# The gated quadrants of a convolution-and-MLP layer: TensorE transposes replaced by transposing transfers

## The reference

```
h = rmsnorm(x, mix_norm)
b, c, v = split(h @ conv_w_in, 3)              # 2048 -> 3 x 2048
u = c * v
y = causal depthwise convolution of u, 3 taps over the tokens
x = x + (b * y) @ conv_w_out
a = relu(rmsnorm(x, mlp_norm) @ mlp_w1)        # 2048 -> 8192
out = x + (a * a) @ mlp_w2                     # 8192 -> 2048
```

## Time and profile before

| what | value |
|---|---|
| median of 3 runs | 1902.61 us (1902.35 to 1905.46) |
| the profiled execution, its own time | 1902.01 us |
| its span | 1900.2 us |
| PE busy | 1892.1 us, 100% |
| DVE busy | 1678.3 us, 88% |
| ACT busy | 1036.5 us, 55% |
| mean busy share of the DMA engines | about 0.7 to 0.9 |
| median landing of a 1 MB weight load issued by SP | 7.5 us |
| PE transposes (L1328) | 392, of them 64 for GATED pairs |

### The profile page before, as it was taken

How to read it: one execution, slowest core, us unless ns; L and a number is a source line. 1 busy time by engine, 2 the same in 40 slices (tenths; PEclk the granted TensorE clock), 3 DMA queues, 4 the chain that set the end, 5 groups by cost and what they waited for, 6 DMA issues and landing times.

```text
span 1900.2 us, 22331 instructions
## 1 busy us (share of the span) xinstructions
PE 1892.1 (100%) x8540; PEld 1568.6 (83%) x8540; DVE 1678.3 (88%) x1500; ACT 1036.5 (55%) x1110; POOL 150.9 (8%) x242
## 2 busy tenths in 40 slices
PE   9999999999999999999999999999999999999999
PEld 8888888888888888888888888888888888888887
DVE  6689899898999898989989899898998889788878
ACT  6464564545558477586675866745444343334432
POOL 0100010000011111120110201100000000000000
PEclk9999999999999999999999999999999999999999
DMA  9774768749676976987968879699988878877783
GB/s 372 263 261 124 265 206 326 234 120 329 216 208 267 354 241 205 338 282 241 357 221 326 288 243 356 222 397 403 357 328 344 346 283 314 352 314 278 294 328 118
DMA packets 137306, 537.87 MB, mean 283 GB/s; under 512 B 27888, under 2 KB 31984, under 8 KB 112240
## 3 DMA queue, kind: packets, MB, share of 16 engines
q1 hardware_dynamic: 103072, 412.65, 56.7%
q0 software_dynamic: 33984, 123.75, 21.3%
q10 hardware_dynamic: 144, 0.04, 0.0%
HBM read 438.35 MB, written 94.37 MB: 280 GB/s over the span
## 4 chain that ended last, share of the span: by engine, by line
PE 68%; DMA 1%; ACT 0%; issue 0%; DVE 0%; SPq 0%; ACTq 0%
PE pair L1293 66%; PE pair L1328 1%; DMA raw<-in_turns 1%; SPq L410 0%; DVE raw L985 0%; ACT sum L695 0%; ACT quads L749 0%; DVE sum_l_mix L1022 0%; ACT ring L651 0%; ACT junk L759 0%; ACT quads L701 0%; DVE x L1100 0%; ACT act L769 0%; ACTq L650 0%; ACTq L360 0%
## 5 line engine op out<-in xcount | busy, mean ns | idle before, releaser
L1293 PE MATMUL pair<-ring,act 128*128 128x512 f32 x7728 | 1767.0, 390 | 1.5 <-issue 1.2
L1293 PEld LDWEIGHTS pair<-ring,act 128*128 128x128 f32 x7728 | 1446.2, 188 | 302.5 <-issue 4.1
L651 ACT ACTIVATE ring<-raw 128x1024 fp32r<-128x1024 f32 x659 | 696.4, 1060 | 798.3 <-PE pair L1293 512.1
L991 DVE TENSOR_TENSOR ring<-raw,ring 128x1024 fp32r<-128x1024 f32 x659 | 792.2, 1221 | 159.1 <-ACT ring L651 156.8
L985 DVE TENSOR_TENSOR raw<-raw 128x1024 f32<-128x1024 f32 x312 | 367.8, 1220 | 9.9 <-DMA raw<-in_turns 1.7
L518 POOL DMA_DIRECT2D spill<-stage x136 | 78.6, 617 | 488.2 <-ACT stage L774 372.8
L531 POOL DMA_DIRECT2D raw<-in_turns x56 | 50.4, 1053 | 701.2 <-DVE raw L985 701.2
L972 DVE TENSOR_TENSOR stage<-quads,stage 128x1024 fp32r<-128x1024 f32 x68 | 83.0, 1221 | 23.8 <-ACT stage L774 23.1
L1306 PE MATMUL pair<-ring,act 128*128 128x512 f32 x384 | 87.3, 389 | 0.0
L1306 PEld LDWEIGHTS pair<-ring,act 128*128 128x128 f32 x384 | 72.0, 188 | 14.9
L774 ACT ACTIVATE stage<-quads 128x1024 fp32r<-128x1024 f32 x68 | 71.5, 1051 | 15.9 <-DVE quads L889 6.2
(11 more groups left out here) (107 smaller groups left out, 527.8 us busy)
## 6 DMA issues: line engine op xcount, KB each, us to landing
raw<-in_turns SPq DMA_DIRECT2D x191, 1024.0 KB, 7.5
act<-spill SPq DMA_DIRECT2D x290, 512.0 KB, 6.8
spill<-stage POOLq DMA_DIRECT2D x136, 512.0 KB, 9.3
act<-act_kept SPq DMA_DIRECT2D x74, 512.0 KB, 7.0
raw<-in_turns POOLq DMA_DIRECT2D x56, 512.0 KB, 8.4
act_kept<-act POOLq DMA_DIRECT2D x28, 512.0 KB, 9.6
x_tok<-in_x SPq DMA_DIRECT2D x4, 1024.0 KB, 14.8
x<-mixed SPq DMA_DIRECT2D x8, 512.0 KB, 18.3
```

Source lines behind the costliest of these rows:

```text
L651: nc.scalar.activation(ring[g % RING][:, 0], raw[:, raw_of(v, s), 2 * (s % 2):2 * (s % 2) + 2, :], ACT.Copy).then_inc(hi_ready, 1)
L991: nc.vector.tensor_tensor(ring[g % RING][:, 1], raw[:, raw_of(v, s), 2 * (s % 2):2 * (s % 2) + 2, :], ring[g % RING][:, 0].bitcast(F32), A ...
L1293: mm = nc.tensor.matmul(bank, stationary, moving, start=(opens and k == 0 and n == 0), stop=(closes and k == NT - 1 and n == 2))
```

## The change

Both quadrants of a GATED pair are now turned over as the fourth quadrant of an UP pair is: planes of half words, a transposing transfer, and ACT puts the halves together, here straight into `u_pad`. PE does no transposes for GATED pairs. On ACT, `put_planes` comes at steps 4 and 6 of turns 2, 4, 8 and 10 (two instructions each), and `take_u` at steps 6 and 8 now waits for the transfer and has two instructions instead of one. At step 6 `take_u` of the first half comes before `put_planes` of the second. SP issues both transfers at the head of its list for the turn, each behind its planes. GATED pairs have planes of their own in the stage buffers. The read of x11 moves from SP's list of turn 31 (behind its first activation load) to the end of its list of turn 32.

```diff
 def by_transfer(q):
-    return KINDS[q] == UP and q < NQP - 1
+    return 2 if KINDS[q] == GATED else int(KINDS[q] == UP and q < NQP - 1)
...
-        planes = at("planes", ACTS2 + 24 * KB, [P, 2, 2 * BW], U16)
-        planes_t = at("planes_t", ACTS2 + 28 * KB, [P, 4 * NT, P], U16)
+        planes = [at(f"planes{i}", where, [P, 2, 2 * BW], U16) for i, where in enumerate((STAGE + 4 * KB, ACTS2 + 24 * KB))]
+        planes_t = [at(f"planes_t{i}", where, [P, 4 * NT, P], U16) for i, where in enumerate((STAGE + 8 * KB, ACTS2 + 28 * KB))]
...
-                    sp.wait_ge(planes_out, 2 * (v // 2 - UP0))
-                    sp.dma_start_transpose(planes_t[:], planes[:].rearrange("p z e -> p (z e)")).then_inc(planes_in, 16)
+                    q = v // 2 - 1
+                    for n in range(TRANSFERS[q], TRANSFERS[q + 1]):
+                        sp.wait_ge(planes_out, 2 * n + 2)
+                        sp.dma_start_transpose(planes_t[KINDS[q] == UP][:], planes[KINDS[q] == UP][:].rearrange(
+                            "p z e -> p (z e)")).then_inc(planes_in, 16)
...
-                        q, place = {L11: ("11", x11), S1: ("21", x21), L12: ("22", x22), S3: ("12", x12)}[j]
-                        load_mixed(q, place)
+                        if j != L11:
+                            q, place = {S1: ("21", x21), L12: ("22", x22), S3: ("12", x12)}[j]
+                            load_mixed(q, place)
+                    if v == V_DOWN and j == L22:
+                        load_mixed("11", x11)
...
-            def put_planes(q):
+            def put_planes(q, m):
-                act.wait_ge(rectified, RECTIFIED[q] + 8)
-                words = sums_of(q)[5][:].bitcast(U16).rearrange("p t (b c z) -> p z b t c", c=P, z=2)
+                if KINDS[q] == GATED:
+                    act.wait_ge(u_formed, FORMED_U[q] + 2 * (m + 1))
+                    act.wait_ge(act_formed, 8)
+                    act.wait_ge(act_lo_ready, direct_done(1, S3))
+                    if q > Z0:
+                        for i in (1, 2):
+                            act.wait_ge(spilled[i], 16 * stage_uses(1, i))
+                else:
+                    act.wait_ge(rectified, RECTIFIED[q] + 2 * m + 2)
+                first, _, _, _, _, l22 = sums_of(q)
+                held = first if KINDS[q] == GATED and m == 0 else l22
+                words = held[:].bitcast(U16).rearrange("p t (b c z) -> p z b t c", c=P, z=2)
...
             def take_u(q, half):
-                act.wait_ge(quad_turned, TURNED[q] + half + 1)
+                act.wait_ge(planes_in, 16 * (TRANSFERS[q] + half + 1))
...
-                o = u_pad[:, :, CW - 1 + HALF * half:CW - 1 + HALF * (half + 1)]
-                nc.scalar.activation(o, by_channels(), ACT.Copy).then_inc(quad_ready, 1)
+                first = 2 * (CW - 1 + HALF * half)
+                words = u_pad[:].bitcast(U16)[:, :, first:first + 2 * HALF].rearrange("p a (t z) -> p z a t", z=2)
+                for z in range(2):
+                    ins = nc.scalar.activation(words[:, z], turned_words(q, z).rearrange("p (a b) t -> p a (b t)", b=2), ACT.Copy)
+                ins.then_inc(quad_ready, 1)
...
+                        if kind == GATED and s in (4, 6):
+                            put_planes(q - 1, s // 2 - 2)
...
-                            at_slot = {3: 0, 5: 1} if KINDS[v // 2 - 1] == GATED else {0: 0, 2: 1, 4: 2, 5: 3}
-                            if s in at_slot and not (at_slot[s] == 3 and by_transfer(v // 2 - 1)):
+                            at_slot = {0: 0, 2: 1, 4: 2, 5: 3}
+                            if s in at_slot and at_slot[s] < 4 - by_transfer(v // 2 - 1) and KINDS[v // 2 - 1] != GATED:
                                 turn_quad(v // 2 - 1, at_slot[s])
```

More of the change, by code:

```diff
@@ L79, in by_transfer @@
 def by_transfer(q):
-    return KINDS[q] == UP and q < NQP - 1
-TURNED = [0]
+    return 2 if KINDS[q] == GATED else int(KINDS[q] == UP and q < NQP - 1)
+TURNED, TRANSFERS = [0], [0]
 for _q, _kind in enumerate(KINDS):
-    TURNED.append(TURNED[-1] + (2 if _kind == GATED else 4 - by_transfer(_q)))
+    TURNED.append(TURNED[-1] + (2 if _kind == GATED else 4) - by_transfer(_q))
+    TRANSFERS.append(TRANSFERS[-1] + by_transfer(_q))
 RECTIFIED = [8 * sum(k in (GATE, UP) for k in KINDS[:q]) for q in range(NQP + 1)]
@@ L657, in place_read @@
                     act.wait_ge(u_formed, FORMED_U[q] + (2, 4, 2, 4)[m])
-                if KINDS[q] != GATED or m in (0, 3):
-                    act.wait_ge(quad_turned, TURNED[q] + ({0: 1, 3: 2}[m] if KINDS[q] == GATED else m + 1))
+                else:
+                    act.wait_ge(quad_turned, TURNED[q] + m + 1)
                 if KINDS[q] == MIXED:
@@ L702, in square_quad, with turned_words @@
                                      pairs[1][:].rearrange("p a t -> p (a t)"), ACT.Square).then_inc(quad_ready, 1)
-            def put_planes(q):
-                act.wait_ge(rectified, RECTIFIED[q] + 8)
-                words = sums_of(q)[5][:].bitcast(U16).rearrange("p t (b c z) -> p z b t c", c=P, z=2)
+            def put_planes(q, m):
[6 more added lines that the diff above has]
+                            act.wait_ge(spilled[i], 16 * stage_uses(1, i))
+                else:
+                    act.wait_ge(rectified, RECTIFIED[q] + 2 * m + 2)
+                first, _, _, _, _, l22 = sums_of(q)
+                held = first if KINDS[q] == GATED and m == 0 else l22
+                words = held[:].bitcast(U16).rearrange("p t (b c z) -> p z b t c", c=P, z=2)
                 for z in range(2):
-                    nc.scalar.activation(planes[:, z].rearrange("p (b t c) -> p b t c", b=NT, t=2), words[:, z],
-                                         ACT.Copy).then_inc(planes_out, 1)
+                    nc.scalar.activation(planes[KINDS[q] == UP][:, z].rearrange("p (b t c) -> p b t c", b=NT, t=2),
+                                         words[:, z], ACT.Copy).then_inc(planes_out, 1)
+            def turned_words(q, z):
+                return planes_t[KINDS[q] == UP][:, 2 * NT * z:2 * NT * (z + 1)]
             def square_planes(q):
-                act.wait_ge(planes_in, 16 * (q - UP0 + 1))
+                act.wait_ge(planes_in, 16 * (TRANSFERS[q] + 1))
                 quads_free(act, q)
@@ L718, in square_planes @@
                 for z in range(2):
-                    nc.scalar.activation(words[:, z], planes_t[:, 2 * NT * z:2 * NT * (z + 1)].rearrange("p a t -> p (a t)"),
+                    nc.scalar.activation(words[:, z], turned_words(q, z).rearrange("p a t -> p (a t)"),
                                          ACT.Copy).then_inc(merged, 1)
@@ L861, in _ @@
                             square_quad(q - 1, {3: 0, 5: 1, 6: 2}[s])
-                        if by_transfer(q - 1) and s == 5:
-                            put_planes(q - 1)
+                        if kind == UP and by_transfer(q - 1) and s == 5:
+                            put_planes(q - 1, 3)
                         if kind == UP and s == 7 and not by_transfer(q - 1):
                             square_quad(q - 1, 3)
-                        if by_transfer(q - 1) and s == 8:
+                        if kind == UP and by_transfer(q - 1) and s == 8:
                             square_planes(q - 1)
@@ L1313, in turn_quad @@
                 kind = KINDS[q]
[L1314 to L1317, removed]
+                o = (first, s1, s4, l22)[m]
+                if kind == MIXED:
                     pe.wait_ge(added, pair_added(q) + FINISHED[m])
@@ L1320, in turn_quad @@
                     pe.wait_ge(rectified, RECTIFIED[q] + 2 * m + 2)
-                if q == 0 and m == 0:
-                    pe.wait_ge(plain_copied, 4)
                 if m > 0:
@@ L1354, in banks_of_product @@
                     else:
-                        pe.wait_ge(quad_ready, TURNS[v // 2] - by_transfer(v // 2 - 1))
+                        if v == PLAIN_TURNS:
+                            pe.wait_ge(plain_copied, 4)
+                        elif KINDS[v // 2 - 1] == GATED:
+                            pe.wait_ge(added, pair_added(v // 2 - 1) + 6)
+                        else:
+                            pe.wait_ge(quad_ready, TURNS[v // 2] - by_transfer(v // 2 - 1))
                 elif u == NC:
```

## The result

| | median us (runs) | span of the profiled execution |
|---|---|---|
| before | 1902.65 (1902.35 to 1905.46, 4) | 1900.2 |
| changed | 1916.06 (1914.60 to 1916.64, 4) | 1914.9 |

The ratio is 1.0066 (95% interval 1.0049 to 1.0083): the change makes the kernel slower by 0.5 to 0.8%, 13.4 us by the medians. The forecast was 1908.6 us, range 1899 to 1918: right in sign and in the chain that costs the time, inside the range, but with less than half of the loss (+6.0 against +13.4), and outside the 1905 to 1912 that it gave as its own spread.

What follows compares the result with a forecast made beforehand. PE was taken to bound the kernel, busy 1892.1 of 1900.2 us. Turns 4, 8, 10 and 2 (+6.5), the moved read (-1.5) and slow transfers (+1.0) made +6.0: 1908.6 us, range 1899 to 1918.

Steps and rivals of the forecast that it cites:

- The removed work, 6.9 us: On PE, eight groups of eight transposes go, priced by pitch at 0.86 us a group, 6.9 us over four turns.
- The chain on ACT: Between hi 6 and hi 7, planes, transfer and takes delay weights; PE waits 4.04 us in turn 4, 2.72 at slot 7.
- The transfer, 3.6 us: Each gated transfer, issued by SP, takes 3.6 us from issue to landing, the median of seven in the trace.
- 1.0 that I allowed: Allowance of 1.0 us for slow transfers among the eight, each standing fully on the path.
- Rival C: All gated transfers land in 4.8 us or more: 9.6 us on the +5.0, 1917 us; chance 0.13.
- Turn 2, -0.95 us: In turn 2 planes start early enough that slot 9 starts at 119.93 against 120.88, 0.95 us shorter.
- SP and the late load of R11, 0: SP's list is held until the second planes; the next turn's R11 load comes 7 us later, costing 0.
- The moved read, -1.5 us: At turn 32 the x11 read no longer stands ahead of weight loads, so PE's 1.50 us wait goes.
- Rival D, the clock: PE's 2.7 us waits bring the 1.2 GHz clock, 8 us over three turns, partly hidden: about 1914; chance 0.06.

Runs made afterwards that it cites:

- e3: Kernel before with one PE transpose of eight kept in each gated group, 56 of 64 left out, no new work: 1898.50 against 1903.30 us, ratio 0.9974.
- e8: e4 with the second half of u formed on DVE at step 4 instead of 3 in turns 4, 8 and 10: 1893.94 against 1902.61 us, ratio 0.9952.
- e0: The changed kernel run again, unedited, as base for other runs: 1915.38 against 1902.41 us for the kernel before, ratio 1.0067.
- e4: Changed kernel with separate plane buffers for the second half, takes at steps 8 and 10, DVE taps later: 1897.44 against 1903.30 us before, ratio 0.9969.
- e5: Changed kernel with each of the eight gated transfers done twice, the second issued when the first has landed: 1955.68 us, ratio to the kernel before 1.0279.
- e6: Changed kernel with one plane of two moved in each gated transfer, half the bytes, values of u wrong: 1907.94 us, ratio to the kernel before 1.0026.
- e1: Kernel before with only the read of x11 put off: 1900.29 against 1903.30 us, ratio 0.9984.
- e9: Changed kernel with sums, quadrants and stage buffers, so the gated planes, 32 bytes further on: 1915.67 us, ratio to the kernel before 1.0064.
- e7: Changed kernel with 20 zero matmuls ahead of PE's wait at slot 7 of turns 4, 8 and 10: 1913.56 us, ratio to the kernel before 1.0056.

## Why the prediction was right, and where it was too small

- **The removed work, 6.9 us.** Held. Leaving out seven eighths gave 4.9 us (e3) where 4.2 was expected after DVE's late lo 4, and e8 fits the full sum. The pitch, not the length of 272 ns, was the right price. One step of the working is off: 23 matmuls that start 0.232 - 0.226 us slower are 0.12 to 0.14 us, not 0.07, which makes a group 0.92 us and the four turns 7.4; no run here can tell that from 6.9. Here the trace speaks against reading the Trainium skill's 275 ns (page "TensorE: Matmul & The Clock Gate", Part 4) as a cost: it is a length, and 64 of those are 17.6 us.
- **The chain on ACT.** Held, step for step. Turn 4 of e0, at full rate, has PE's waits at slots 4, 7, 8 and 9 as 0.26, 3.01, 0.60 and 1.12 us, where 0.36, 2.72, 0.69 and 0.16 were worked out; the 1.12 is the second transfer, 5.2 us from issue to take in place of 3.6. Hi 7 was forecast at 192.45 + 1.33 (the shift of turn 2) = 193.78 us and came at 194.41 in the first execution; PE's wait at slot 7 was forecast as 2.72 us and was 3.04. Taking the chain apart (e4) turned +13 us into about -6 with the same instructions, so neither ACT's added work nor the landing time is to blame in itself: the chain cost about 19 us (e0 against e4). ACT's busy share of 55% was no evidence of room in these five slots.
- **The transfer, 3.6 us: the term that was mis-sized.** The price came from transfers in the UP turns. The gated ones took 4.3 to 5.3 us, each fully on the path. From issue to take the eight of the changed kernel sum to 36.9 us, and doing each twice added 40.3 us (e5), 1.1 us of time per us. Above 8 x 3.6 = 28.8 that is 8 us more, against 1.0 that I allowed. With 8 in the place of 1.0 the sum is +13, and +13.4 was measured. Rival C (all at 4.8 us, 1917 us, chance 0.13) was thus the nearest to what happened. That the time lies in the range is owed to C's place in it, not to the term. e6 tests the same term from the other side: 9.6 us less idle time, 7.4 us less. The Trainium skill's 1309 ns for one 128x128 tile by transfer ("VectorE: DVE Perf Modes", "The three transpose paths") isn't what a transfer of 16 tiles costs per tile here: 4.3 us for all of them.
- **Turn 2, -0.95 us.** It turned out +1.2: the first transfer landed 5.3 us after its issue there (103.29 to 108.57), against the 0.1 us of margin that I had.
- **SP and the late load of R11, 0.** Held: from turn 2 to turn 12 ACT waits for a weight load once, in turn 7. It does so in the kernel before (3.19 us), in the changed one (3.94) and in e5 (4.11), where SP's list is held longer still. It never does in the turns right behind a gated one.
- **The moved read, -1.5 us.** Held, as far as e1's interval tells (1.3 to 4.8 us).
- **Rival D, the clock.** Its first half came true: the lower level was granted in or soon behind waits of 3.0 to 3.6 us, though not behind each of them (once of three times in e0). Its price did not. 10.3 us more at half rate went with 1.4 us more time (e0), since PE at full rate then waits for lo 8 and lo 9. I had put 8 us on it, "partly hidden"; nearly all of it was.

## What to carry to other kernels

Moving work from the bounding engine to an idle one pays only if the idle engine's list has room at that place. Read the list in order, and look for what an in-order engine has queued behind each new wait: here the weights queued behind the transfers cost about 19 us (e0 against e4), nearly three times the 6.9 us of removed work. Give both halves their own buffers, issue both, and do other slots' work before the first take. Price a transfer by its own kind in its own stretch, and where it is on the path, put its spread into the sum.

## What was not expected of the hardware

The same transposing transfer of 0.5 MB moved at 215 GB/s in turn 4 and at 290 in turn 18. Its issue took 1.8 to 2.1 us in seven of the eight gated ones (3.1 in one), and 1.6 to 1.7 in five of the seven UP ones (2.6 and 2.8 in two). Moving the buffers by 32 bytes didn't change the rate (e9), and the cause is open. The granted clock isn't the same from one execution to the next of one kernel (13.7 and 3.4 us at the lower level), and 20 matmuls of 128 columns in a gap didn't prevent its fall in two turns of three (e7). Finally, PE loses more than the idle time that a profile shows, since the idle time counts from the modelled end of a matmul (0.39 us) and the pitch is 0.227. In e4 384 matmuls run from 94.86 us for 87.20, so the next was due at 94.86 + 384 x 0.227 = 181.9; it starts at 182.25, 0.3 us late, where the trace shows 0.19 idle.
